# Feed-forward blocks in two phases of seven-product 2x2x2 tiles, with the gated product kept in DRAM between them

## The reference, cut

```python
def rmsnorm(x, g, eps=NORM_EPS):
    x32 = x.astype(jnp.float32)
    y = x32 * lax.rsqrt(jnp.mean(x32 * x32, axis=-1, keepdims=True) + eps)
    return (y * g.astype(jnp.float32)).astype(x.dtype)
...
def modulate(h, shift, scale):
    return h * (1.0 + scale[:, None, :]) + shift[:, None, :]
...
def swiglu(h, w1, w3, w2):
    return (jax.nn.silu(h @ w1) * (h @ w3)) @ w2
...
    c_act = jax.nn.silu(c)
...
        mod = c_act @ w_ada[l] + b_ada[l]
        sh1, sc1, gt1, sh2, sc2, gt2, sh3, sc3, gt3 = jnp.split(mod, N_MOD, axis=-1)
        h = modulate(rmsnorm(x, g_ffn1[l]), sh1, sc1)
        x = x + 0.5 * gt1[:, None, :] * swiglu(h, ffn1_w1[l], ffn1_w3[l], ffn1_w2[l])
        h = modulate(rmsnorm(x, g_mix[l]), sh2, sc2)
        x = x + gt2[:, None, :] * hybrid_mixer(
...
        h = modulate(rmsnorm(x, g_ffn2[l]), sh3, sc3)
        x = x + 0.5 * gt3[:, None, :] * swiglu(h, ffn2_w1[l], ffn2_w3[l], ffn2_w2[l])
    modf = c_act @ w_ada_final + b_ada_final
    shf, scf = jnp.split(modf, 2, axis=-1)
    return modulate(rmsnorm(x, g_final), shf, scf)
```

## Time and profile before

| | |
|---|---|
| runs | 2086.07, 2090.1, 2091.6 us; median 2090.1 |
| profiled execution, span | 2089.5 us |
| PE busy | 1994.5 us, 95% |
| DVE, ACT, POOL busy | 49%, 25%, 7% |
| mean granted PE clock | 0.977 |
| DMA | 146.80 MB, mean 70 GB/s |

### The profile page before, as it was taken

The page is one execution under the profiler, slowest core; times in us unless marked ns, Lnnn a source line. Parts: engine busy times, 40 slices in busy tenths (PEclk is TensorE's granted clock), DMA queues, the critical chain, the costliest instruction groups (busy, mean ns, idle before and its releaser), DMA issues.

```text
span 2089.5 us, 23956 instructions
## 1 busy us (share of the span) xinstructions
PE 1994.5 (95%) x8992; PEld 1616.5 (77%) x8992; DVE 1020.9 (49%) x1404; ACT 528.8 (25%) x865; POOL 137.5 (7%) x154
## 2 busy tenths in 40 slices
PE   5999999999999999999998887799999999999997
PEld 2788888888888887888876665588888888888886
DVE  4854544554554337444235777752444324443246
ACT  3311121111111126211135455541111111111115
POOL 2000000000000001000312330000000000000001
PEclk8899999999999999999999999899999999999998
DMA  7523243224321110111211110011111111111102
GB/s 289 177 95 111 100 132 109 94 89 139 117 94 51 41 61 21 52 40 51 71 41 36 46 40 11 21 41 51 50 40 54 47 50 50 40 54 46 50 31 81
DMA packets 43442, 146.80 MB, mean 70 GB/s; under 512 B 5504, under 2 KB 5888, under 8 KB 43264
## 3 DMA queue, kind: packets, MB, share of 16 engines
q1 hardware_dynamic: 26064, 91.24, 12.6%
q0 software_dynamic: 12672, 46.14, 6.4%
q10 hardware_dynamic: 4656, 8.73, 1.4%
HBM read 137.70 MB, written 4.19 MB: 68 GB/s over the span
## 4 chain that ended last, share of the span: by engine, by line
PE 88%; DVE 5%; ACT 2%; issue 2%; DMA 1%; ACTq 1%; POOL 0%; DVEq 0%; POOLq 0%
PE PS L1000 87%; DMA X<-x_t 1%; DVE X L734 1%; PE PS L1315 1%; DVE Wl L644 1%; DVE NMax L914 1%; DVE TmpA L703 0%; DVE SqSum L685 0%; ACT DT L601 0%; DVE PS L912 0%; DVE XN L812 0%; DMA Ada<-ada 0%; DVE AdaSum L662 0%; ACT Hh L431 0%; ACT Out L374 0%
## 5 line engine op out<-in xcount | busy, mean ns | idle before, releaser
L1000 PE MATMUL PS<-Hh,Wh 128*128 128x512 f32 x1728 | 683.2, 395 | 9.6 <-DVE Hl L708 8.1
L1000 PE MATMUL PS<-Hl,Wh 128*128 128x512 f32 x1728 | 677.1, 392 | 0.0
L1000 PE MATMUL PS<-Hh,Wl 128*128 128x512 f32 x1728 | 677.1, 392 | 0.0
L734 DVE SCALAR_TENSOR_TENSOR X<-PS,Gate,X 128x512 f32<-128x512 f32 x448 | 329.3, 748 | 193.3 <-PE PS L1000 193.1
L1000 PEld LDWEIGHTS PS<-Hh,Wh 128*128 128x128 f32 x1728 | 327.0, 189 | 90.8 <-issue 11.3
L1000 PEld LDWEIGHTS PS<-Hh,Wl 128*128 128x128 f32 x1728 | 327.1, 189 | 69.2
L1000 PEld LDWEIGHTS PS<-Hl,Wh 128*128 128x128 f32 x1728 | 327.6, 190 | 66.2
L1000 PE MATMUL PS<-Gh,Wh 128*128 128x512 f32 x832 | 331.2, 398 | 13.6 <-DVE X L734 11.8
L1000 PE MATMUL PS<-Gh,Wl 128*128 128x512 f32 x832 | 325.7, 391 | 0.0
L1000 PE MATMUL PS<-Gl,Wh 128*128 128x512 f32 x832 | 325.6, 391 | 0.0
L644 DVE TENSOR_TENSOR Wl<-Wr,Wh 128x1024 fp32r<-128x1024 f32 x164 | 201.4, 1240 | 247.3 <-ACT Wh L348 247.2
(11 more groups left out here) (114 smaller groups left out, 1107.8 us busy)
## 6 DMA issues: line engine op xcount, KB each, us to landing
Wr<-units SPq DMA_DIRECT2D x164, 512.0 KB, 3.2
Ada<-ada POOLq DMA_DIRECT2D x80, 512.0 KB, 4.5
AdaFirst<-ada POOLq DMA_DIRECT2D x8, 512.0 KB, 11.5
X<-x_t ACTq DMA_DIRECT2D x8, 512.0 KB, 13.5
out_t<-Out SPq DMA_DIRECT2D x16, 256.0 KB, 2.0
TmpA<-TmpA ACTq DMA_DIRECT2D x48, 64.0 KB, 2.0
Rope<-rope SPq DMA_DIRECT2D x1, 1024.0 KB, 10.0
...
```

The costliest lines, as they stand in the source:

```text
L734: nc.vector.scalar_tensor_tensor(X[:, d, half(h)], PS[:, bank, :], Gate[:, n, d:d + 1], X[:, d, half(h)], ALU.mult, ALU.add).then_inc(evac, 1)
L1000: return nc.tensor.matmul(out, lhs, rhs, start=first, stop=last)
```

## The change

It touches both FFNs, how X, weights and the ada tiles are loaded, and little of the attention and convolution (whose loops are unrolled and whose buffers become Mh, Ml, Mr, Hh[h] and Hl[h], with the same instructions).

**Up phase.** h @ w1 and h @ w3 are made for all of D_FF first. A unit u = 0 to 21 is one group and one of w1, w3. Its weights form 2x2 blocks (2 slices of D_FF by 2 halves of the features) and the activations 2x2 blocks (2 halves of the features by 2 of the tokens). Units 0 and 1 are made the plain way (`plain_group`, 8 products of 24 matmuls). For each of the 20 others, seven block products, 12 matmuls each (4 k-tiles x 3), are made instead of eight; their operands are blocks or sums and differences of blocks. That is 192 + 20 x 7 x 12 = 1872 matmuls where there were 2112. Products are counted by t; one of the 20 x 7 is unit u, place j.

The sums of activations are made once, in place in X, by DVE (`t_add`, 128x1024), with ACT and DVE splitting them (`t_hi`, `t_lo`); X itself is normalised in place before that (`nm` on DVE, `b_chunk` with two ACT instructions, `b_chunk_lo` on DVE). The sums of weights are made by DVE for four places of seven (`raw_sum`, L916 to L926, 128x512). The weights of a product are prepared five products ahead (AHEAD) into 8 slots of 128x512 (`prep_hi` on ACT, `prep_lo` on DVE, L908). Two banks of one unit take all seven products: some products go on in the bank of an earlier one, and in between ACT copies the bank to T (places 0 to 2) or DVE adds the bank to T (places 3 to 5, L964); units take the three bank pairs of 0 to 5 in turn. ACT makes silu in T, DVE the gated product into T[4+q] (L974), one 128x512 quadrant q of two slices x two halves at a time.

SP stores each quadrant to `g_dram` (256 KB, L369). DVE makes the sums of w2's blocks in the same phase (`w2_op`, L986, 44 of 128x512); POOL loads w2's blocks and stores the sums to `s_dram`. Ada tiles run in both up phases: six sections in the first (Ada ring of two), three in the second.

**Down phase.** G @ w2 is made as seven products over the whole of D_FF, each 11 steps of 12 matmuls (924, where there were 1056). The four quadrants of G, 44 blocks of 256 KB, come back over POOL's queue into GQ, which lies where the weights and activation sums of the up phase lay; SP loads w2's blocks or sums (`load_down`, 256 KB, a ring of 8). For each step ACT makes two high parts (`down_hi`), DVE two low parts and in four of the seven products a difference of quadrants first (`down_lo`, L937, L940, L943). X was overwritten, so SP loads it again, 4 transfers of 1 MB with rows of 2 KB (L408), from x_t in the first FFN and from x_dram, to which it is stored after the attention, in the second. After each product DVE adds the banks to X (`x_add`, L1079).

**Norm at the end of an FFN.** The half-0 quadrants are finished first; mean and broadcast of half 0 stand in product 6 at steps 2 and 6, and the chunks of half 0 are normalised from step 7 on. Product 6 is the last quadrant of half 1: after it four times an add to X, a square and an add of squares, then the mean of half 1, which in the first FFN stands in `project_new`, after chunk 5.

**Start.** X comes in rows of 2 KB; AdaSecond, 4 transfers of 1 MB, takes all of section SC1; 4 x 512 KB of raw weights follow the first X blocks. All eight weight preparations and the sixteen `nm` stand ahead of the scale.

```diff
+PAIRS = 2 * NG
+SLOTS = 8
+AHEAD = 5
+AHEAD_B = 3
+N_UP = 8 + 7 * (PAIRS - 2)
+N_DOWN = 7 * NG
+N_FFN = N_UP + N_DOWN
+X_BANKS, Y_BANKS = (0, 1, 3, 2), (4, 5, 6, 7)
...
+DOWN_TO = ((0, 1), (1, 0), (0, 0), (0, 0), (1, 0), (0, 1), (1, 1))
+DOWN_G = (1, 1, 1, 2, 0, 3, 1)
+DOWN_SUM = {1: (0, 1), 2: (2, 1), 4: (2, 0), 6: (3, 1)}
+SUM_COUNT = {1: 0, 2: 1, 4: 2, 6: 3}
+LOADS = {1: 1, 0: 2, 2: 3, 3: 4}
+PLACE_OF_SUM = {1: 3, 2: 0, 3: 1, 4: 2}
...
+        def operand(h, k):
+            return ((0, 5), ("B12", 3))[h][k // KH], k % KH
...
+                    sp.dma_start(flat(Raw[:, n, :, :]), up_w[ph, u, f]).then_inc(up_loaded[n], 16)
+            def spill(ph, g, q):
+                sp.wait_ge(mul_done, silu_no(ph, g, q))
+                sp.dma_start(g_dram[ph][g, q], T[:, 4 + q, :]).then_inc(spilled[q], 16)
...
+                    if t == N_UP - AHEAD:
+                        for m in range(8):
+                            load_down(ph, m)
+                spill(ph, NG - 1, Q_OF_J[6])
+                sp.wait_ge(prod, N_FFN * ph + N_UP)
+                for n, (k, h) in enumerate(((0, 1), (KH, 0), (0, 0), (KH, 1))):
+                    x = x_dram if ph else x_t
+                    if ph:
+                        for kk in range(k, k + KH, 2):
+                            sp.wait_ge(x_stored[kk // 2], 16 * NH)
+                    sp.dma_start(X[:, h, k:k + KH, :], x[h, k:k + KH].rearrange("k p s -> p k s"))\
...
+                for m in range(8, N_DOWN):
+                    load_down(ph, m)
...
+                    x = (t - 10) // 3
+                    if t >= 10 and (t - 10) % 3 == 0 and x < 4 * NG:
+                        n = (3, 2, 0, 1)[x % 4]
+                        pool.wait_ge(w2_sum, 4 * NG * ph + x + 1)
+                        pool.dma_start(s_dram[ph][x // 4, n], W2s[:, n, :]).then_inc(w2_stored[n], 16)
+                        if n == 1 and x // 4 + 1 < NG:
...
+                    pool.wait_ge(spilled[q], 16 * (NG * ph + g + 1))
+                    if e >= NG or ph:
+                        pool.wait_ge(gq_loaded[g], 16 * (4 * ph + e // NG))
+                    pool.dma_start(GQ[q][:, g, :], g_dram[ph][g, q]).then_inc(gq_loaded[g], 16)
...
+                plain_silu(ph, 0)
+                plain_silu(ph, 2)
+                t_hi(ph, 0, 1)
+                t_hi(ph, 1, 2)
+                for o in (8, 9, 10):
+                    prep_hi(ph, o)
+                t_hi(ph, 2, 4)
+                plain_silu(ph, 1)
+                plain_silu(ph, 3)
+                t_hi(ph, 3, 6)
+                for o in (11, 12):
+                    prep_hi(ph, o)
+                for t in range(8, N_UP):
...
+            def raw_sum(ph, u, j):
+                out = source(u, j)
+                if j == 1:
+                    for f in range(GF):
+                        dve.wait_ge(up_loaded[2 * (u % 2) + f], 16 * (NG * ph + u // 2 + 1))
+                    nc.vector.tensor_tensor(out, raw_of(u, 2), raw_of(u, 3), ALU.add).then_inc(summed, 1)
...
+            def up_evict(ph, t):
+                u, j = 2 + (t - 8) // 7, (t - 8) % 7
+                g, w = u // 2, u % 2
+                x = 2 * ((u - 2) % 3)
...
+                    dve.wait_ge(acopy, acopy_no(ph, u, {3: 2, 4: 1, 5: 0}[j]))
+                    nc.vector.tensor_tensor(T[:, 4 * w + q, :], T[:, 4 * w + q, :], PS[:, x + (j != 4), :], ALU.add)\
+                        .then_inc(dadd, 1)
...
+                nc.vector.tensor_tensor(W2s[:, out, :], W2s[:, a, :], W2s[:, b, :], op).then_inc(w2_sum, 1)
...
+                nc.vector.tensor_tensor(X[:, h, k, :], X[:, h, k, :], PS[:, 7 - h, :], ALU.mult).then_inc(nm_done, 1)
...
+                for t in range(8, N_UP):
+                    if t + AHEAD < N_UP:
+                        prep_lo(ph, t + AHEAD)
+                    elif t + AHEAD_B >= N_UP:
+                        down_lo(ph, t + AHEAD_B - N_UP)
+                    if t > 8:
+                        up_evict(ph, t - 1)
+                    if t >= 10 and (t - 10) % 3 == 0 and (t - 10) // 3 < 4 * NG:
+                        w2_op(ph, (t - 10) // 3)
...
+                if i in (0, 1, 2, 6):
+                    dve.wait_ge(xq_loaded[{0: 0, 1: 1, 2: 2, 6: 3}[i]], 16 * (ph + 1))
+                else:
+                    dve.wait_ge(x_added, 28 * ph + 4 * {3: 2, 4: 1, 5: 0}[i] + d + 1)
+                nc.vector.scalar_tensor_tensor(X[:, h, k, :], PS[:, (Y_BANKS if i % 2 else X_BANKS)[d], :],
+                                               Gate[:, 2 * ph, k:k + 1], X[:, h, k, :], ALU.mult, ALU.add)\
...
+                for d in range(KH):
+                    x_add(ph, 6, d)
+                    add_squares(q + 1, KH + d)
+                spread(q + 1)
...
+            def up_free(ph, u, j):
+                if j == 0:
+                    if u < 5:
+                        pe.wait_ge(silu_done, silu_no(ph, 0, (0, 2, 1)[u - 2]))
+                    elif u % 2:
+                        pe.wait_ge(silu_done, silu_no(ph, (u - 3) // 2, 2))
+                    else:
+                        pe.wait_ge(mul_done, silu_no(ph, (u - 3) // 2, 2))
+                elif j == 1:
+                    if u < 5:
+                        pe.wait_ge(mul_done, silu_no(ph, 0, (0, 2, 1)[u - 2]))
+                    else:
+                        pe.wait_ge(dadd, dadd_no(ph, u - 3, 5))
+                elif j < 5:
+                    pe.wait_ge(acopy, acopy_no(ph, u, j - 2))
+                else:
+                    pe.wait_ge(dadd, dadd_no(ph, u, j - 2))
...
+                for t in range(8, N_UP):
+                    u, j = 2 + (t - 8) // 7, (t - 8) % 7
+                    bank = 2 * ((u - 2) % 3) + (j in (1, 3, 5))
+                    ada_between(ph, t)
+                    pe.wait_ge(w_lo, N_FFN * ph + t + 1)
+                    if u == 2 and j in (1, 2, 4, 6):
+                        pe.wait_ge(b_lo, 24 * ph + {1: 18, 2: 20, 4: 22, 6: 24}[j])
+                    up_free(ph, u, j)
+                    fresh, last = j in (0, 1, 5), j in (3, 5, 6)
+                    for k in range(KH):
+                        w = blk(k)
+                        mm_open(PS[:, bank, :], Wh[:, t % SLOTS, w], Bh[j][:, k, :], fresh and k == 0, False)
+                        mm_open(PS[:, bank, :], Wh[:, t % SLOTS, w], Bl[j][:, k, :], False, False)
+                        made = mm_open(PS[:, bank, :], Wl[:, t % SLOTS, w], Bh[j][:, k, :], False, last and k == KH - 1)
+                    made.then_inc(prod, 1)
...
+                    if i == 6 and g == 2:
+                        pe.wait_ge(x_added, 28 * ph + 23)
+                        mean(q)
+                    if i == 6 and g == 6:
+                        bcast(q)
+                    pe.wait_ge(w_lo, N_FFN * ph + N_UP + m + 1)
+                    pe.wait_ge(gt_lo, N_DOWN * ph + m + 1)
+                    for d in range(KH):
+                        bank = (Y_BANKS if i % 2 else X_BANKS)[d]
+                        if g == 0:
+                            down_free(ph, i, d)
+                        w, b = 4 + m % 4, m % 4
+                        mm_open(PS[:, bank, :], Wh[:, w, blk(d)], Wh[:, b, :], g == 0 and i in (0, 1, 5), False)
+                        mm_open(PS[:, bank, :], Wh[:, w, blk(d)], Wl[:, b, :], False, False)
+                        made = mm_open(PS[:, bank, :], Wl[:, w, blk(d)], Wh[:, b, :], False, g == NG - 1 and i in (3, 5, 6))
+                        if g == NG - 1 and d < KH - 1:
```

More of the change, by code:

```diff
@@ L39 @@
 KT = D // P
+KH = KT // 2
 HALF = 512
@@ L54 @@
 RING = 3
-ADA_RING = 4
 BANKS = 6
@@ L1000, in mm, with mm_open, ada_between @@
                 return nc.tensor.matmul(out, lhs, rhs, start=first, stop=last)
+            def mm_open(out, lhs, rhs, first, last):
+                return nc.tensor.matmul(out, lhs, rhs, start=first, stop=last, skip_group_check=True)
+            def ada_between(ph, t):
+                for y in range(KT - 1, KT * len(ADA_IN[ph]), KT):
+                    if ada_step(ph, y) + 2 == t:
+                        if y == KT - 1:
+                            pe.wait_ge(silu_done, silu_no(ph, 0, 3))
+                        ada_cols(ADA_IN[ph][y // KT])
```

1140 lines of the change are left out of this document (712 added, 428 removed).

## The result

The changed kernel takes 2028.73 us, median of 4 runs (2025.92 to 2030.84), against 2088.19 of the kernel before measured beside it (4 runs): a ratio of 0.9708, 95% interval 0.9693 to 0.9723. It is 59 us faster; the prediction's sum was 112.6, and the time lies above the range that was given. The profiled execution has a span of 2024.1, where the sum of the prediction gave 1976.9: 47.2 are missing.

What follows compares the result with a forecast made beforehand. PE, busy 95% of the span, was taken to bound the kernel. Fewer matmuls (−168.6) and added costs, chiefly at the start and phase changes, summed to −112.6 against 2089.5: 1976.9 in the profile, 1977 forecast; range 1951 to 2005.

Steps and rivals of the forecast that it cites:

- Matmuls: Both FFNs: 744 fewer matmuls in all, each at a pitch of 0.2266 us, all on PE's path; −168.6 us.
- Up to down: Changeover in both FFNs: X's reload delays the ninth weight block, PE stalls 4.5 plus 1.5 at half clock; +12, bounds 0, 20.
- Start: Kernel start: queues share by packets, X's last byte at 42.2, first matmul at 80.8; +22 us, bounds +12 and +25.
- Behind the plain products: First seven-product unit: PE stands 3.4 for ACT's bank copy, loses 1.0 at half clock; +8.8 for two FFNs, bounds 0, 12.
- Steady state: Up phase: DVE has 28.0 of 38.1 us of work, weights five products ahead, so little shows; +2 us.
- Rivals 2 and 3: Up phase: DVE runs late, +28, 2003, chance 0.15; or the eviction chain paces PE at 3.13 a product, 2092, chance 0.04.
- First FFN to convolution: Behind the first FFN: half 0 normalised at +12.5, mean of half 1 at +20.7, PE waits 9.8; +8, bounds 3, 11.
- Attention to second FFN: From the last add to X after attention to the second FFN's start at 1353.3, against 1348.4; +4.9, bounds 2 and 8.
- The last product of the up phase: End of each up phase: it must be evicted before the down phase takes its bank; 0.6 each, +1.2 us.
- The end: From the second FFN's end to the kernel's end: 19.3 before, 19.75 now; +0.5 us.
- number 1: Start and changeover are covered: start costs 12.6, X's reload hides behind the eight blocks; 1956 us, chance 0.20.
- Number 4: DMA streams of 256 KB instead of 512 KB transfers run at 0.341 MB/us, delaying start and reload; 1993 us, chance 0.06.

Runs made afterwards that it cites:

- run 1: Changed kernel with the pad 256 bytes instead of 64, so all PE operands start at the same place within 256 bytes; 2008.52 us.
- runs 3 and 4: Changed kernel with X's reload spread behind later down-phase weight blocks, 1988.82 us; the same plus equal operand addresses, 1967.46 us.
- run 3: Changed kernel with X's four 1 MB reloads behind down-phase weight blocks 10, 14, 22 and 30, not all ahead of block 8; 1988.82 us.
- Run 8: Changed kernel with equal addresses and spread reload, plus AdaSecond's transfers held until block 6 of X has landed; 1957.09 us.
- Run 10: Changed kernel with equal addresses, spread reload, overlapped tail, later AdaSecond, plus ACT's copy of product 8 ahead of high parts 12 to 14; 1945.65 us.

## Why the prediction was wrong, by its steps

**Matmuls, −168.6.** Right in number, wrong in price. The count is 8248. This is one of the two steps that failed: it took the pitch of before, 0.2266, for every matmul of the new code, where the seven-products of the up phases went at 0.2320 on average, and an argument from full clock and the absence of waits had nothing in it that could see an address. Equal addresses brought 20.2 back in the time. Between their first matmul and the first of the down phase the changed kernel and run 1 differ by 9.9 in the first FFN and 9.3 in the second, runs 3 and 4 by 10.7 and 8.9: some 19 us in either pair, for a line in the diff that the prediction passed over. Between the FFNs, where Mh lies 64 bytes off Hh and Hl, the first pair differs by −0.7 and the second by 3.7, so there no cost is clear of the scatter of single profiles.

**Up to down, +12.** The mechanism was right and the size was not: 35 of waits and some 5 at half clock behind them, in place of 12. The ninth weight block was to be there 26.3 after the last product; it came after 38 (540.27 + 27.11 = 567.38 against 529.4). The step that failed here is "At half of 0.410 MB/us they take 20.5". DMA between 533 and 567, all and by queue, and the median time to landing of X's 1 MB:

```profile
DMA packets 5123, 13.12 MB, mean 386 GB/s; under 512 B 607, under 2 KB 607, under 8 KB 5122
...
q0 software_dynamic: 2364, 7.72, 60.1%
q1 hardware_dynamic: 2758, 5.39, 43.4%
...
X<-x_t SPq DMA_DIRECT2D x4, 1024.0 KB, 20.7
```

X's queue (q1) got 5.39 MB of 13.12, 0.159 MB/us, and not 0.205. The other queue, with the loads of G, passed 2364 packets against 2758 but 7.72 MB: its packets are 3.3 KB, those of q1 2.0 KB. That is the sharing by packets that the step *Start* had read from the earlier trace rows and used, and that this step forgot. X's last MB landed at 565.3, 32.6 after the first was issued, in place of 20.5, and the next three weight blocks landed almost with it, at 567.4, 567.8 and 568.5. At 0.159 MB/us X and these three (4.98 MB) take 31.3 of the 34.7 us from 532.68 to 567.38; where the other 3 went is open. The upper bound of 20 was too low for the same reason.

The changeover cost 40 by run 3, 28 more than forecast, and the addresses 20 by run 1: 48 together, against 47.2 missing. The errors of the other steps cancel within a few us, which is luck: the start came out 6 cheaper than forecast, and the step behind the first FFN and the end some 3 and 4 dearer.

**Start, +22.** The first matmul was forecast at 80.8 and came at 77.50. X's last byte was forecast at 42.2 and came at 40.97, where sharing by bytes would have given 32.6. Run 8 turned the mechanism round, and X came at 28.05. One reading behind the sum was wrong: the FFNs of before were taken to end at 798.2 and 2070.2, but output jobs still followed. Their last output matmuls are these:

```profile
800.50 0.39 PE L1000 MATMUL PS<-Gh,Wl 128*128 128x512 f32 x1
...
2072.53 0.39 PE L1000 MATMUL PS<-Gh,Wl 128*128 128x512 f32 x1
```

So the first ended at 800.7 and began in effect at 63.6, and the start cost 3.3 less than forecast and then 2.5 less again, about 16. The second ended at 2072.8. Such an error moves cost from the step ahead of an FFN to the one behind it and leaves the sum as it is.

**Behind the plain products, +8.8.** Waits of 2.7 in each FFN were found, 3.4 forecast, and the copy on ACT is what ends them. Run 10 got back 4.4 of the 8.8.

**Steady state, +2.** There is no wait of PE between product 11 and the end of either up phase. Rivals 2 and 3 did not occur: with DVE 80% busy in the stretch shown (40.22 of 50) preparing five products ahead was enough. The sign that was named for them, a pitch of the seven-products above 2.8, was all but reached (2.80 in place of 2.72), and for a reason that neither of them has.

**First FFN to convolution, +8.** Half 0 was to be normalised 12.5 after the last matmul, the mean of half 1 to come 20.7 after it. It came at 782.83 − 761.69 = 21.1. PE waited 12.6 in the projections ahead of it, in three pieces (1.85, 2.44, 8.36), where 9.8 was forecast. With the end of the FFN before put right (800.7), the cost up to the first mean of a convolution group is 11.1 (PE takes it at 809.76, 48.1 behind the FFN, and took it at 837.64, 36.9 behind), at the upper bound.

**Attention to second FFN, +4.9.** Right in the stretch that it counted. From the last add to X to the first matmul 10.3 were forecast, 5.2 before and 5.1 more. DVE's last add ahead of the second FFN is this one:

```profile
1313.12 0.74 DVE L1200 SCALAR_TENSOR_TENSOR X<-PS,Gate,X 128x512 f32<-128x512 f32 x1
```

The first matmul follows at 1323.54, 10.4 later. From the end of the first FFN to the first matmul of the second it was 545.0 and is 561.8, 16.8 longer: 11.1 was there at the first group mean, 5.3 comes here, and 0.4 is left for all between.

**The other terms.** The last product of the up phase cost 0.9 and 0.7, 0.6 forecast. The end, from the last matmul of the second FFN on, was 16.7 (2089.5 − 2072.8) and is 20.9 (2024.1 − 2003.2): +4.2 in place of +0.5. Of that 2.6 is the wrong reading of 2070.2, and PE's wait for the last mean is 6.3 long where it was 3.0. Of the rivals, number 1 (the reload of X is covered) went the wrong way altogether. Number 4, slower small transfers, did not show: DMA ran at 386 GB/s in the changeover, and with the order changed that was enough. By the Trainium skill, "DMA: Bandwidth & Descriptors", section "Measured (HBM→SBUF, 128 partitions, SWDGE, issued from GpSimd)", 341 GB/s belongs to single transfers of 1 MB; several in flight passed 386 here with blocks of 256 KB among them, so its figure is no ceiling for transfers that overlap.
